# Value sums of the sample requests moved into the attention phase of a one-layer decoder step

## The reference, cut to what matters

```python
# branch B: 12 heads of 64 in three groups of 4; 128 cached rows of each group, gathered by stride
p = jnp.exp(logits - lse[..., None])
out = jnp.einsum('bhtj,btjhc->bthc', p, kv[:, :, :, 1])      # value sum, per group
o = jnp.einsum('gbth,gbthc->bthc', softmax(lses), outs)      # groups combined: 4 heads of 64 remain
# branch C: 4 heads of 128 over 256 memory rows
p = jax.nn.softmax(logits, axis=-1)
out = jnp.einsum('bhtm,bmhc->bthc', p, mem_kv[:, :, 1])
# all rows
merged = sig(g_A)*(a_out @ w_branch_a) + sig(g_B)*(b_out @ w_branch_b) + sig(g_C)*(c_out @ w_branch_c)
x = x + merged @ w_out
```

## Time and profile before

| | |
|---|---|
| Median of 3 runs | 1539.71 us (1538.79 to 1542.64) |
| The profiled execution | 1539.54 us, of which 1537.7 us are the span of the trace |
| Mean granted TensorE clock | 0.953 |
| Busy: PE, PE weight load, DVE, ACT, POOL | 92%, 45%, 24%, 16%, 3% |
| Chain that ended last | PE 65%, DMA 21%, DVE 5%, SP's queue 4% |
| DMA | 515.17 MB, mean 335 GB/s |
| DMA queues | q1 (SP and ACT) 493.69 MB, q0 (POOL) 18.83 MB |

### The profile page before, as it was taken

One profiled execution on the slowest core, in us unless ns is written; L12 is line 12 of the kernel. 1 busy time (PEld: TensorE's weight loads), 2 busy tenths in 40 slices (PEclk: granted clock), 3 DMA queues, 4 the chain that ended last, 5 costly groups with the idle time before them and its releaser, 6 DMA issues.

```text
span 1537.7 us, 20357 instructions
## 1 busy us (share of the span) xinstructions
PE 1409.7 (92%) x8013; PEld 693.9 (45%) x8013; DVE 374.8 (24%) x858; ACT 240.7 (16%) x389; POOL 52.6 (3%) x90
## 2 busy tenths in 40 slices
PE   3999977997898779999999999999999999999995
PEld 1685535866786334343343433333343333333333
DVE  2100365420012152222222212222221222222123
ACT  2001011220001041121111111111121111112112
POOL 0100212002100000000000000000000000000000
PEclk9999877996599989999999999999999999999998
DMA  9535966239247657999999999999999999999994
GB/s 319 181 128 191 328 236 237 89 157 345 94 163 288 261 207 310 424 422 421 422 422 422 421 423 421 422 422 422 422 422 422 422 422 422 421 422 422 422 422 164
DMA packets 86697, 515.17 MB, mean 335 GB/s; under 512 B 10047, under 2 KB 11655, under 8 KB 36812
## 3 DMA queue, kind: packets, MB, share of 16 engines
q1 hardware_dynamic: 77504, 493.69, 79.3%
q0 software_dynamic: 6016, 18.83, 3.8%
q10 hardware_dynamic: 3148, 2.24, 0.5%
HBM read 511.21 MB, written 47.52 MB: 363 GB/s over the span
## 4 chain that ended last, share of the span: by engine, by line
PE 65%; DMA 21%; DVE 5%; SPq 4%; issue 2%; ACT 1%; ACTq 1%; POOL 0%; DVEq 0%
PE psum L524 62%; DMA weights<-in_w_gate_up 17%; SPq L424 4%; PE psum L527 3%; DMA weights<-in_w_out 2%; DMA weights<-in_cache_mem_kv 2%; DVE qk L1272 1%; ACTq L1325 1%; ACT qk L1328 0%; POOL weights L484 0%; DVE x L1297 0%; DVE kvt L1166 0%; DVE va L1179 0%; DVE hT L1242 0%; DVE kc L1177 0%
## 5 line engine op out<-in xcount | busy, mean ns | idle before, releaser
L524 PE MATMUL psum<-weights,wsp 128*64 128x512 f32 x2048 | 491.8, 603 | 15.2 <-DMA weights<-in_w_gate_up 14.4
L524 PE MATMUL psum<-weights,merged 128*64 128x512 f32 (+2 forms) x1152 | 274.3, 600 | 10.7 <-DMA weights<-in_w_out 9.2
L524 PEld LDWEIGHTS psum<-weights,wsp 128*64 128x64 f32 x2048 | 127.5, 136 | 266.8 <-issue 177.9
L1242 DVE TENSOR_TENSOR hT<-psum,hT 128x264 f32<-128x264 f32 x264 | 101.7, 427 | 529.4 <-PE psum L524 529.3
L524 PE MATMUL psum<-hT,weights 128*128 128x264 f32 x704 | 171.7, 403 | 13.8 <-DVE weights L984 9.1
L524 PEld LDWEIGHTS psum<-weights,merged 128*64 128x64 f32 (+2 forms) x1152 | 89.6, 141 | 167.0 <-issue 158.9
L524 PEld LDWEIGHTS psum<-hT,weights 128*128 128x128 f32 x704 | 138.2, 198 | 45.6 <-DVE weights L984 12.2
L524 PE MATMUL psum<-bT,merged 64*128 64x264 f32 x528 | 94.2, 434 | 1.1 <-ACT merged L1487 0.7
L1468 ACT COPY bT<-psum 128x264 f32<-128x264 f32 x33 | 12.5, 379 | 484.1 <-PE psum L527 484.0
L524 PEld LDWEIGHTS psum<-bT,merged 64*128 64x128 f32 x528 | 39.8, 184 | 106.7 <-issue 103.9
L1272 DVE TENSOR_SCALAR qk<-psum,lowest 128x512 f32<-128x512 f32 x64 | 48.0, 750 | 162.6 <-PE psum L524 159.2
(11 more groups left out here) (242 smaller groups left out, 765.3 us busy)
## 6 DMA issues: line engine op xcount, KB each, us to landing
weights<-in_w_gate_up SPq DMA_DIRECT2D x256, 1024.0 KB, 26.1
weights<-in_w_down SPq DMA_DIRECT2D x128, 1024.0 KB, 25.0
out<-in_cache_win_kv SPq DMA_DIRECT2D x8, 4094.0 KB
weights<-in_w_in SPq DMA_DIRECT2D x13, 2048.0 KB, 7.7
weights<-in_cache_mem_kv POOLq DMA_DIRECT2D x16, 512.0 KB, 7.8
out<-in_cache_win_kv SPq DMA_DIRECT2D x2, 4088.0 KB
weights<-in_cache_win_kv POOLq DMA_DIRECT2D x48, 128.0 KB, 6.1
weights<-in_w_mem_kv SPq DMA_DIRECT2D x2, 2048.0 KB, 14.4
```

The costliest lines, as they stand in the source:

```text
L524: return nc.tensor.matmul(out, lhsT, rhs, start=start, stop=stop, **kw)
L1242: V.tensor_tensor(acc[:, c, :], p_a[j % 2][part], acc[:, c, :], ALU.add).then_inc(s_acc, 1)
```

## The change

The step `sv` is gone. In its place there are four rounds of two samples each. `svb` and `svc` of a round stand at the end of iterations 7, 11, 15 and 17 of the attention phase. The probabilities (4 columns) are now stationary and the value rows move (256 columns for branch B, three products that add up over the groups; 512 columns for branch C, two products). The two samples of a round write to output rows 32 apart, rounds 0 and 2 at rows 0 and 32, rounds 1 and 3 at 64 and 96, as separate column tiles of the array. ACT copies each result to `mixed_s` (L1423). Every two rounds PE turns the result back (`svbt`, `svct`: 2 and 4 transposes), and DVE picks four columns at a stride of 32 out of each. Four samples are done in iteration 13, four after the last iteration.

POOL loads the values of samples 0 and 1 as before, right behind the keys. The values of round r > 0 wait for the `svc` of round r-1, since both buffers are read there.

Heads of branch B now lie in pairs over 128 rows in `bT`, so that `p` of branch B is 2 products with 128 rows where it was 4 with 64. `vts` takes 6 transposes in place of 12.

```diff
@@ schedule
+VALUE_ROUNDS = {7: 0, 11: 1, 15: 2, 17: 3}
         if n == 4:
             s += [("ssum",)]
-    for b in range(NS):
-        s += [("sv", b)]
+        if n in VALUE_ROUNDS:
+            s += [("svb", VALUE_ROUNDS[n]), ("svc", VALUE_ROUNDS[n])]
+        if n == 13:
+            s += [("svbt", 0), ("svct", 0)]
+    s += [("svbt", 1), ("svct", 1)]
@@ build
-        bT = bT_all[0:HD, :].rearrange("p (h t) -> p h t", h=HPG)
+        bT = bT_all[:, 0:2 * NT].rearrange("p (j t) -> p j t", j=2)
@@ SP
                     sp.wait_ge(s_mixed, 2 * (CH + HPG))
-                    taken(sp, "sv", NS - 1)
+                    taken(sp, "svct", 1)
@@ POOL
+            def values(b):
+                if b < ROUND:
+                    pool.wait_ge(s_kv_used, NS - 1 + b)
+                else:
+                    pool.wait_ge(s_job, job[("svc", b // ROUND - 1)] + 1)
+                stream(1, b, kv_b[b % ROUND], kv_c[b % ROUND], s_valin[b % ROUND])
@@ PE
                     else:
-                        taken(pe, "sv", NS - 1)
-                        last = wide_tile(o[:, 0:NT], weights("wb"), m, bT, HPG)
+                        taken(pe, "svbt", 1)
+                        last = wide_tile(o[:, 0:NT], weights("wb"), m, bT, 2)
-                    for h in range(HPG):
-                        for g in range(NG):
-                            hh = g * HPG + h
-                            mm(o[0:HD, h:h + 1], kv_b[b % 2][:, g, h * HD:(h + 1) * HD], pb[:, b, hh:hh + 1], g == 0, g == NG - 1)
-                    for h in range(CH):
-                        for j in range(2):
-                            last = mm(o[:, HPG + h:HPG + h + 1], kv_c[b % 2][:, j, h * P:(h + 1) * P], pc[:, b, j, h:h + 1],
-                                      j == 0, j == 1)
+                elif kind == "svb":
+                    for i in range(ROUND):
+                        pe.wait_ge(s_valin[i], 64 * (r + 1))
+                    for g in range(NG):
+                        for i in range(ROUND):
+                            at = 32 * (r % 2 * ROUND + i)
+                            last = mm(o[at:at + HPG, 0:HPG * HD], pb[:, r * ROUND + i, g, :], kv_b[i][:, g, :], g == 0, g == NG - 1)
+                elif kind == "svc":
+                    for t in range(2):
+                        for i in range(ROUND):
+                            at = 32 * (r % 2 * ROUND + i)
+                            last = mm(o[at:at + CH, 0:CH * CD], pc[:, r * ROUND + i, t, :], kv_c[i][:, t, :], t == 0, t == 1)
+                elif kind in ("svbt", "svct"):
+                    pe.wait_ge(s_smix, 2 * r + (1 if kind == "svbt" else 2))
+                    for i in range(cn):
+                        last = turn(o[:, i * P:i * P + rows], mixed_s[:, c0 + i * P:c0 + (i + 1) * P], rows)
@@ ACT
+                elif kind in ("svb", "svc"):
+                    act.wait_ge(s_job, n + 1)
+                    A.copy(mixed_s[at, c:c + w], o[at, 0:w]).then_inc(free, 1)
```

More of the change, by code:

```diff
@@ L51 @@
 CHUNKS = KD + KD // 2
+ROUND = 2
+HALF = NS // 2
+VALUE_ROUNDS = {7: 0, 11: 1, 15: 2, 17: 3}
 USED = CHUNKS - 2
@@ L155 @@
 ROTATING = {"vec", "wsp", "rel", "sbias", "memT", "kc", "xT", "vc", "kct", "q", "k", "v", "kt", "qc", "qs", "qcs", "vts",
-            "selfb", "sk", "skc", "zv", "zu", "vat", "sp", "p", "g", "ssum", "sv", "wos", "wo", "woz", "xt", "rt", "lg", "pos"}
+            "selfb", "sk", "skc", "zv", "zu", "vat", "sp", "p", "g", "ssum", "svb", "svc", "svbt", "svct", "wos", "wo", "woz", "xt", "rt", "lg", "pos"}
 LAST_USE = {("kc", 3): 0, ("vc", 1): 1, ("q", 3): 2, ("k", 1): 3, ("k", 5): 4, ("v", 2, 0): 5, ("v", 2, 1): 6, ("qc", 3): 7,
@@ L263, in build @@
         sself = sb("sself", [P, NS * NH])
-        vts = sb("vts", [HD, NH, NS])
-        vself = sb("vself", [HD, HPG, NS])
+        vts = sb("vts", [P, NH // 2, NS])
+        vself = sb("vself", [P, 2, NS])
         th = [sb(f"th{n}", [P, NT]) for n in range(2)]
@@ L336, in build @@
         s_kvin = [sem(f"kv_in{n}") for n in range(2)]
+        s_valin = [sem(f"values_in{n}") for n in range(ROUND)]
+        s_smix = sem("sample_mix")
         s_kvout, s_kvcout, s_vaout = sem("out_kv"), sem("out_memkv"), sem("out_chunk_v")
@@ L501, in _ @@
                     pool.dma_start(O[6 + g][0, :, w - 1, a].rearrange("b h c -> b (h c)"), rows[0:NS, 2, c]).then_inc(s_kvout, 16)
-            for n in range(2, NS + 2):
-                stream(n)
+            for b in range(2, NS):
+                keys(b)
+            for b in range(ROUND):
+                values(b)
             pool.wait_ge(s_done["va"], 1)
@@ L507, in _ @@
             nc.gpsimd.partition_all_reduce(smax[:], samp[:], P, bass.bass_isa.ReduceOp.max).then_inc(s_done["parmax"], 1)
-            for n in range(NS + 2, 2 * NS):
-                stream(n)
+            for b in range(ROUND, NS):
+                values(b)
             pool.wait_ge(s_job, job[("rt",)] + 1)
@@ L623, in _ @@
                     taken(pe, "v", 2, 1)
-                    for h in range(NH):
-                        last = turn(o[0:HD, h * NS:(h + 1) * NS], v_tok[0:NS, 2, h * HD:(h + 1) * HD], NS)
+                    for i in range(NH // 2):
+                        last = turn(o[:, i * NS:(i + 1) * NS], v_tok[0:NS, 2, i * P:(i + 1) * P], NS)
                 elif kind == "selfb":
@@ L652, in _ @@
                     elif br_ == "c":
-                        taken(pe, "sv", NS - 1)
+                        taken(pe, "svct", 1)
                         pe.wait_ge(s_mixout, 2 * (CH + HPG))
@@ L971, in _ @@
                     ready()
-                    V.tensor_copy(vts[:], o[0:HD, 0:NH * NS].rearrange("p (h b) -> p h b", h=NH)).then_inc(free, 1)
+                    V.tensor_copy(vts[:], o[:, 0:NH // 2 * NS].rearrange("p (i b) -> p i b", i=NH // 2)).then_inc(free, 1)
                     own()
@@ L1073, in _ @@
                     dve.sem_inc(s_done["sprob"], 1)
[L1075 to L1079, removed]
-                    ready()
-                    seq(V.tensor_tensor(bT[:, :, SEQ + b:SEQ + b + 1], o[0:HD, 0:HPG].unsqueeze(2), vself[:, :, b:b + 1], ALU.add))
-                    V.tensor_copy(qcT[:, :, SEQ + b:SEQ + b + 1], o[:, HPG:HPG + CH].unsqueeze(2)).then_inc(free, 1)
-                    dve.sem_inc(s_kv_used, 1)
+                    for half in range(2):
+                        r = slice(half * HD, (half + 1) * HD)
+                        pf = sself[r, :].rearrange("p (b i a) -> p a i b", b=NS, a=2)[:, half, :, :]
+                        seq(V.tensor_tensor(vts[r, :, :], vts[r, :, :], pf, ALU.mult))
+                    seq(V.tensor_reduce(vself[:], vts[:].rearrange("p (g j) b -> p j b g", g=NG), AX.X, ALU.add))
+                elif kind in ("svbt", "svct"):
+                    r, = a
+                    ready()
+                    at, to = n % 3 * 512, slice(SEQ + r * HALF, SEQ + (r + 1) * HALF)
+                    if kind == "svbt":
+                        for half in range(2):
+                            hs = slice(half * HD, (half + 1) * HD)
+                            picked = psum[hs, at + half:at + half + 2 * (P + 2)].rearrange("p (j x) -> p j x", j=2)[:, :, 0:32 * HALF:32]
+                            ins = V.tensor_tensor(bT[hs, :, to], picked, vself[hs, :, r * HALF:(r + 1) * HALF], ALU.add)
+                            if half == 0:
+                                seq(ins)
+                        ins.then_inc(free, 1)
+                    else:
+                        picked = psum[:, at:at + CH * (P + 1)].rearrange("p (h x) -> p h x", h=CH)[:, :, 0:32 * HALF:32]
+                        V.tensor_copy(qcT[:, :, to], picked).then_inc(free, 1)
                 elif kind == "score":
@@ L1372, in _ @@
                     A.activation(va[0:tn, t, :], o[0:tn, :], ACT.Gelu_apprx_tanh).then_inc(free, 1)
+                elif kind in ("svb", "svc"):
+                    c, w = (0, HPG * HD) if kind == "svb" else (HPG * HD, CH * CD)
+                    act.wait_ge(s_job, n + 1)
+                    if kind == "svb" and a[0] == 2:
+                        taken(act, "svct", 0)
+                    at = slice(64 * (a[0] % 2), 64 * (a[0] % 2) + 32 * (ROUND - 1) + HPG)
+                    A.copy(mixed_s[at, c:c + w], o[at, 0:w]).then_inc(free, 1)
+                    if a[0] % 2 == 1:
+                        act.wait_ge(free, n // 3 + 1)
+                        act.sem_inc(s_smix, 1)
                 elif kind == "zu":
```

40 lines of the change are left out of this document (23 added, 17 removed).

## The result

The changed kernel takes 1530.15 us (median of 4 runs, 1527.68 to 1531.21), the kernel before beside it 1539.25 (4 runs, 1538.56 to 1542.64). The ratio is 0.9932, with a 95% interval from 0.9913 to 0.995: 9 us faster (8 to 13 by the interval), where 14.4 were forecast. The profiled execution took 1531.21 us, its span 1529.3.

What follows compares the result with a forecast made beforehand. Experts were taken as bound by weight DMA (422 GB/s), so their earlier start counts one for one. Branch C starting 12.6 us earlier plus 1.8 of clock gave 14.4 us: 1539.7 to 1525.3, range 1512 to 1537.

Steps and rivals of the forecast that it cites:

- The rounds: PE's added products per round of two samples, two abreast on column tiles: 3.4 us a round at full clock.
- The rival of 6.2 us: Rounds' products not abreast on column tiles: 6.2 us for 3.4, 8.4 us more in all, 1533.7 us; chance 0.07.
- The wait of round 1: PE waits 22 us (bounds 0 and 26) for values 2 and 3, held up by the four-engine shift, landing at 341.5.
- The landing's own delay: Allowance for the round 1 loads' landing after their remaining packets, included in the 341.5 us landing time.
- Clock after a wait: PE's lower clock after waiting for values adds 1.5 us, so round 1 takes 4.9 us instead of 3.4.
- Round 2: Its values, issued at 346.4 with no shift on the way and needed 30 us later, cause no wait.
- The wait of round 3: PE waits 8.3 us for the last values, issued at 387.8 beside SP's x and gb0, landing at 396.5.
- The chain behind round 3: Uncovered steps before branch C: ACT 0.6, four transposes 0.5, DVE 0.2, handovers 0.6 us.
- The slower rival: Round 3's loads meet the 4.1 MB shift and land 36.3 us after 388.2; 1553 us; chance 0.08.
- The start of branch C: First product of branch C at 403.3 instead of 415.9 us, 12.6 us gained, plus 1.8 from full clock.
- Branch B and `w_out`: Branch B's halved products save 6 us net, but the `w_out` wait grows from 9 to 15: counted 0, at most 6.
- What was said of the experts: From 700 to 1500 us experts run at their weights' DMA rate, whatever PE does; an earlier start counts one for one.

Runs made afterwards that it cites:

- e1: Changed kernel with each four-sample shift of the middle window issued as four one-sample shifts over all 16 DMA engines: 1489.07 us, ratio 0.9662.
- e3: Changed kernel with rounds 0 and 1 at iterations 5 and 7 instead of 7 and 11, so their loads precede the shift: 1510.28 us, ratio 0.9786.
- e8: Changed kernel with each four-sample shift of the middle window as two DMAs of 1 KB rows, still on four engines: 1513.38 us in a single run.
- e5: Changed kernel with branch B's product issued four times instead of twice per block, its sum counted double: 1531.66 us, ratio 0.9924.
- e6: e1's kernel with branch B's product issued four times instead of twice, as in e5: 1491.12 us, ratio 0.9665.
- e9: e1's kernel run again, beside e10 on one chip: 1488.49 us, ratio 0.9654.
- e10: e6's kernel run again, beside e9 on one chip: 1491.38 us, ratio 0.9675.
- e4: Changed kernel with round 2 at iteration 13 instead of 15, so the last values load earlier: 1517.78 us, ratio 0.9846.
- e7: Changed kernel with both the one-sample shifts of e1 and round 2 at iteration 13 as in e4: 1476.6 us, ratio 0.9574.

## Why the prediction was right, and where its sizes were off

- *The rounds:* 3.18 us where 3.4 were counted; two products abreast on tiles with 4 stationary columns cost no more than on the tile width of the earlier trace rows. The rival of 6.2 us is out.
- *The wait of round 1:* 22.62 us for 22, landing at 344.3 for 341.5 with the round itself begun later. e1, e3 and e8 each change the meeting with the shift in another way (all engines for four; loads ahead of it; packets of 1 KB), and each time the wait is gone or 2.7 us. The mechanism is shown. The landing's own delay, about 1 us of the forecast's sum, was an estimate with no row behind it: after, the last packets of POOL's queue start at some 343.6 us, and PE goes on at 344.35.
- *Clock after a wait:* the two levels are 0.50 (380 to 400 us of the kernel before) and 1.00 (420 to 440). Round 1 takes 4.57 for 3.18, 1.4 us for the 1.5 counted. The windows after (columns as in the earlier trace rows) have a granted clock of 0.68 in the 5 us behind either wait:

```profile
344.00:349.00 5.00, 4.65 (x21) 1.30 (x22) 0.00 (x0) 0.40 (x2) 0.00 (x0) 0.68 0.00 0
402.00:407.00 5.00, 4.79 (x22) 1.34 (x22) 0.00 (x0) 0.45 (x2) 0.00 (x0) 0.68 1.03 360
```

- *Round 2:* no wait, as forecast.
- *The wait of round 3:* this term was mis-sized. 12.13 us for 8.3. The last value load was issued at 390.1, with SP's x in the same instant, and landed 12.0 us later; the earlier trace rows had 8.7 for a load behind x and gb0. A pair of samples was on its way in both cases. POOL's queue just ahead of the last issue, before (357 to 363.9 us) and after (386 to 390.1):

```profile
q0 software_dynamic: 29, 0.10, 4.0%
...
q0 software_dynamic: 53, 0.17, 16.0%
```

  Of the pair's 1.8 MB, 1.7 were still to come in either kernel, and in the next 6 us POOL's queue moved 1.3 MB in either. So the pair ahead isn't the difference; the last 0.4 MB come later, beside x and the small loads that SP issued in the same instant and not 10 us earlier. Why is open. The same wait is 10.7 to 15.6 us in e1, e3, e5, e6, e8, e9 and e10; e4 and e7 show that it goes, and is worth its 12 to 13 us, when the load is issued one stage earlier. The slower rival named the same place: its price of 36 us did not come, since the load was through ahead of the 4.1 MB piece.
- *The start of branch C:* 408.5 for 403.3. Of the 5.2 us, 3.8 are round 3's wait. Another 2.4 stood already at 293.2, where SP issued wc at 290.8 before: PE was 1.5 us later at 29 us (29.89 for 28.43), far ahead of the change. Round 0 began at 293.78 here, and at 291.22, 293.00, 293.06 and 293.81 in e4, e7, e8 and e5, which are the same up to there. So this is the spread from one execution to the next. The terms between (0.73 for 0.8, shorter rounds, the turns) give about 1 back. The chain behind round 3 was counted as 1.9 us; its 0.2 for DVE and 0.6 for handovers were estimates with no row behind them. From the end of the round (406.86) to branch C (408.53) it took 1.7.
- *Branch B and `w_out`:* 15.23 us for 15. From the start of branch C to `wos` PE takes 92.4 us where it took 99.3: 1.8 are the clock of the first products and 5.1 branch B's, where 6 were counted (the wait in its middle grew from 4.69 to 6.73 us, as forecast, and the products behind it ran 0.8 us longer). The product behind the wait for `w_out` came only 8.2 us earlier, though the shift on which it hangs went out 9.25 earlier (461.18 to 451.93). o1 itself was issued 10.4 us earlier, but took 37.6 us to land where it took 35.4. That o1 lay behind the shift on four engines stands in the trace of before. From 310 to 320 us (the busy share and GB/s in 40 slices of 0.25 us, for the row) the packets start four at a time, every 2.4 us: 1047 GB/s are four of 64 KB in a slice. While o1 was on its way, from 500 to 505 us, nothing but such a shift moved (columns as in the earlier trace rows):

```profile
DMA  0000000090000000009000000006900000000900
GB/s 0 0 0 0 0 0 0 0 1047 0 0 0 0 0 0 0 0 0 1047 0 0 0 0 0 0 0 0 262 785 0 0 0 0 0 0 0 0 1047 0 0
```

```profile
500.00:505.00 5.00, 5.00 (x22) 3.77 (x21) 0.86 (x2) 0.39 (x1) 0.00 (x0) 1.00 0.24 105
```

  After, it is the same from 495 to 505 us (0.24, 105 GB/s). e5 shows no loss when branch B pays as before, within what the runs can tell.
- *The sum:* the end moves as the start of the experts does: 8.0 us at the second product behind `w_out`, 8.4 in the span, and 9.1 by the medians. The 14.4 of the forecast are 5.2 too many at the start of branch C, and one more at `w_out`. What was said of the experts was too broad, though. Up to 860 us PE is as full as the DMA engines; only behind that does it wait for weights. Windows after (us; busy of PE, PEld, DVE, ACT, POOL; clock; DMA share; GB/s):

```profile
700.00:860.00 160.00, 159.31 (x1052) 62.60 (x1050) 35.76 (x83) 29.32 (x42) 0.00 (x0) 1.00 1.01 422
860.00:1500.00 640.00, 623.08 (x3976) 232.40 (x3974) 140.88 (x327) 105.42 (x152) 0.00 (x0) 1.00 1.01 422
```

It made no difference here, since both start with the first expert.
- *A reading:* the row of 12.33 us holds 80 rows, which are 40 products and two samples. So two samples took 12.3 us at the low clock (0.50 from 380 to 400 us) and take 3.18 in a round at the full one.

## What to carry to other kernels

Before a load is put in a new place, list what the other queues will have on the way at that moment, and with what packets: 62 us of serial work were taken off PE, and the waits for two loads gave 35 of them back. Look for a transfer whose share of the 16 engines stands at a quarter while little else moves; issuing it in copies that use all engines was worth more here (41 us) than the change under study. When a saved stage ends in a wait for data, its worth is read only after that wait is gone: the same change gave 9 us before the shift was spread and 40 after.

## What the runs showed of the hardware

- A copy from HBM to HBM with 4 as its outer dimension ran at the share of four of 16 engines (24.1%), four packets of 64 KB at a time and 2.4 us each, at 105 GB/s; issued as four copies of one sample each it used all engines (86.2% of their time beside the other queue's 18.2%), in packets of 64 KB too, and the loads beside it landed after 17.5 us instead of 42.8.
- With 64 KB packets on one queue and packets of up to 4 KB on the other, the two queues moved the same number of packets: 16 and 16 in 10 us on four engines; in e1, on all engines, 62 and 64 in 6 us.
- With 1 KB rows the copy moved 0.97 MB in 10 us at a share of 27.1%, but the other queue's loads landed in 7.3 us. SP was held for 28.2 and 37.7 us by two such shifts (two DMAs each), where the other form took 0.7, and then for 21.6 us by the load of `w_out`.
